# Layer 1's fifth modulation chunk, moved from the second attention to the boundary between the layers

## The reference, cut to what matters

```python
for l in range(DEPTH):                      # DEPTH = 2
    mod = (silu(c) @ w_ada[l] + b_ada[l])   # 6 x 1024 values, and the same for c_ctx
    sh1, sc1, gt1, sh2, sc2, gt2 = jnp.split(mod, 6, axis=-1)
    h = modulate(rms_norm(x, g_mix[l]), sh1, sc1)
    ... = split_in(h @ w_in[l])             # conv, neighbourhood attention, windowed attention, gates
    x = x + gt1 * merge_branches((o_a, o_b, o_c), (ga, gb, gc), w_branch[l], w_out[l])
    h = modulate(rms_norm(x, g_ffn[l]), sh2, sc2)
    x = x + gt2 * expert_choice_ffn(h, w_router[l], w_exp_gate[l], w_exp_up[l], w_exp_down[l])
```

## Time and profile before

| what | value |
|---|---|
| median of 3 runs | 1836.38 us (1835.15 to 1837.97) |
| the profiled execution | 1836.14 us, span 1834.3 us |
| TensorE busy | 1686.4 us, 92% |
| VectorE busy | 765.9 us, 42% |
| ScalarE busy | 476.6 us, 26% |
| read from HBM | 539.13 MB, 296 GB/s over the span |

### The profile page before, as it was taken

The page is one execution under the profiler, slowest core; times in us unless marked ns, Lnnn a source line. Parts: engine busy times, 40 slices in busy tenths (PEclk is TensorE's granted clock), DMA queues, the critical chain, the costliest instruction groups (busy, mean ns, idle before and its releaser), DMA issues.

```text
span 1834.3 us, 26452 instructions
## 1 busy us (share of the span) xinstructions
PE 1686.4 (92%) x10822; PEld 974.9 (53%) x10822; DVE 765.9 (42%) x1742; ACT 476.6 (26%) x1048; POOL 109.5 (6%) x149
## 2 busy tenths in 40 slices
PE   5999999999998999999998799999999998787876
PEld 3887777776664333333232498877882332222222
DVE  3455566665424233332323665577753222111111
ACT  4224455552133100000000535555441000000001
POOL 1101210000001000000000012200000000000000
PEclk9999999999998999999999999999999999999988
DMA  9533231127778999999999774247899999999997
GB/s 351 159 92 95 84 92 58 37 79 262 268 274 350 409 428 427 428 428 427 428 427 427 275 226 132 76 132 261 284 366 381 426 426 426 427 424 426 426 426 288
DMA packets 149987, 543.83 MB, mean 296 GB/s; under 512 B 10026, under 2 KB 88304, under 8 KB 124652
## 3 DMA queue, kind: packets, MB, share of 16 engines
q1 hardware_dynamic: 147056, 535.35, 74.5%
q0 software_dynamic: 2400, 6.16, 1.3%
q10 hardware_dynamic: 412, 0.64, 0.1%
HBM read 539.13 MB, written 2.98 MB: 296 GB/s over the span
## 4 chain that ended last, share of the span: by engine, by line
PE 67%; DMA 25%; DVE 3%; ACT 2%; SPq 1%; issue 1%; POOL 0%; DVEq 0%; ACTq 0%
PE bank L2193 19%; PE bank L2053 11%; PE bank L2054 10%; PE bank L2055 10%; DMA ring<-in_w_exp_gate 8%; DMA ring<-in_w_exp_down 8%; DMA ring<-in_w_exp_up 5%; DMA spare<-in_w_exp_gate 3%; PE bank L1952 2%; PE bank L2082 2%; PE bank L2106 2%; PE bank L2167 2%; PE bank L2092 2%; PE bank L2222 1%; DMA ring<-in_w_in 1%
## 5 line engine op out<-in xcount | busy, mean ns | idle before, releaser
L2193 PE MATMUL bank<-ring,XEP 128*32 128x256 f32 (+1 forms) x2384 | 385.3, 618 | 32.0 <-DMA ring<-in_w_exp_gate 15.5
L2053 PE MATMUL bank<-HH,WH 128*128 128x512 f32 (+1 forms) x800 | 286.4, 358 | 4.8 <-DVE HL L1642 4.0
L2054 PE MATMUL bank<-HL,WH 128*128 128x512 f32 (+1 forms) x800 | 275.4, 344 | 0.0
L2055 PE MATMUL bank<-HH,WL 128*128 128x512 f32 (+1 forms) x800 | 274.9, 344 | 0.0
L2193 PEld LDWEIGHTS bank<-ring,XEP 128*32 128x32 f32 (+1 forms) x2384 | 114.7, 130 | 272.3 <-issue 226.4
L1614 DVE TENSOR_TENSOR WL<-ring,WH 128x1024 fp32r<-128x1024 f32 (+1 forms) x172 | 184.6, 1076 | 139.9 <-ACT WH L1373 139.1
L1874 DVE TENSOR_TENSOR X<-X,bank 128x512 f32<-128x512 f32 x184 | 113.9, 681 | 185.9 <-PE bank L2222 100.2
L1373 ACT CAST WH<-ring 128x1024 fp32r<-128x1024 f32 (+1 forms) x172 | 158.0, 926 | 126.4 <-PE bank L2055 64.7
L2193 PE MATMUL bank<-ring,HIDT 128*32 128x256 f32 (+1 forms) x1232 | 153.0, 479 | 31.1 <-DMA ring<-in_w_exp_down 31.1
L2053 PEld LDWEIGHTS bank<-HH,WH 128*128 128x128 f32 x800 | 151.7, 190 | 50.0 <-issue 26.7
L2055 PEld LDWEIGHTS bank<-HH,WL 128*128 128x128 f32 x800 | 151.8, 190 | 18.5
(11 more groups left out here) (251 smaller groups left out, 2050.8 us busy)
## 6 DMA issues: line engine op xcount, KB each, us to landing
ring<-in_w_exp_gate SPq DMA_DIRECT2D x55, 2048.0 KB, 31.0
ring<-in_w_exp_up SPq DMA_DIRECT2D x49, 2048.0 KB, 34.7
ring<-in_w_exp_down SPq DMA_DIRECT2D x48, 2048.0 KB, 36.3
ring<-in_w_ada SPq DMA_DIRECT2D x48, 1024.0 KB, 7.6
ring<-in_w_in SPq DMA_DIRECT2D x40, 1024.0 KB, 8.3
split_slot<-in_w_exp_up SPq DMA_DIRECT2D x8, 2048.0 KB, 29.1
split_slot<-in_w_exp_down SPq DMA_DIRECT2D x8, 2048.0 KB, 33.3
ring<-in_w_in SPq DMA_DIRECT2D x28, 512.0 KB, 5.2
```

The lines of the kernel that those rows point to most:

```text
L2053: mm(t, wh, hi[:, k, 0:b.n], start=k == 0, stop=False)
L2054: mm(t, wh, lo[:, k, 0:b.n], start=False, stop=False)
L2055: last = mm(t, wl, hi[:, k, 0:b.n], start=False, stop=k == b.kk - 1)
L2193: last = mm(out_bank[tw * g:tw * g + tw, 0:nw], stationary(k), w[:, g::G] if spread else w[:, nw * g:nw * g + nw], start=k == 0, stop=k == ...
```

## The change

Chunk 4 of layer 1 is no longer made in the second attention. Its two pieces are loaded between the two loads of the first products ("ac"), at the layer's head. TensorE multiplies the first half (four matmuls) into bank 3 ahead of the turns, once four of the last eight additions to X are done, and the second half behind the first five turns. VectorE copies it after the first two product blocks, and its transposes follow the third. The second attention's four pairs then carry chunks 5, 6, 7 and 8, one each; before they carried 4, then 5 and 6, then 7, then 8.

```diff
+GT1_0 = 2 * GT1
+    def boundary_ada(l, c, pieces):
+        mm = P.tile(dve=True, bank=3)
+        for ch in pieces:
+            ch.used_tile = mm.ready
+        return Step(kind="ada", layer=l, l=l, v=c // 2, half=c % 2, chunk=pieces, tile=mm, buffer=0)
...
-            return [P.load([(0, (8, 256), ("w_in", l, COL[name] + 256 * r, 256))]) for r in range(2)]
+            between = []
+            if last and name == "ac":
+                between = [(0, (4, 512), ("w_ada", l, 512 * GT1_0, 512, 4 * r, 4)) for r in range(2)]
+            first, second = [(0, (8, 256), ("w_in", l, COL[name] + 256 * r, 256)) for r in range(2)]
+            loaded = [P.load([part]) for part in [first] + between + [second]]
+            return loaded[:1] + loaded[-1:], loaded[1:-1]
+
+        boundary = None
+        if l == 0:
+            turns = turn_steps(0, KD // 2)
+        else:
+            first_ac, pieces = col_chunk("ac")
+            turns = turn_steps(0, 5)
+            boundary = boundary_ada(l, GT1_0, pieces)
+            turns += turn_steps(5, KD)
...
                 elif turns:
+                    P.add("ada_part", ada=boundary, halves=(0,))
                     P.steps[l] += turns[:5]
+                    P.add("ada_part", ada=boundary, halves=(1,))
                     for k, (one, two) in enumerate(zip(ksteps(P, head), ksteps(P, b))):
...
                     run([("done", head), ("done", b)])
+                    P.add("ada_out", ada=boundary)
+                    turn_ada(boundary)
...
-                now = ((4,), (5, 6), (7,), (8,))[p]
-                sums = sums[:mid] + [("call", ada(l, now[0]))] + sums[mid:] + [("call", ada(l, c)) for c in now[1:]]
+                sums = sums[:mid] + [("call", ada(l, GT1_0 + 1 + p))] + sums[mid:]
...
+                    elif kind == "ada_part":
+                        if 0 in s.halves:
+                            pe.wait_ge(x_added, ADD0[l] - ADDS[l - 1] + 4)
+                        modulation(s.ada, s.halves)
```

More of the change, by code:

```diff
@@ L96, with __init__ @@
 class Step:
-    def __init__(self, ac_tile=None, act=None, after_expert=None, arrive=None, arrived=None, at=None, b=None, bank=None, before=None, bias=None, buffer=None, casts=None,
+    def __init__(self, ac_tile=None, act=None, ada=None, halves=None, after_expert=None, arrive=None, arrived=None, at=None, b=None, bank=None, before=None, bias=None, buffer=None, casts=None,
                  bias_before=None, blk=None, br=None, c_tile=None, chunk=None, code=None, col=None, d=None, d_tile=None,
@@ L109, in __init__ @@
         self.act = act
+        self.ada = ada
+        self.halves = halves
         self.after_expert = after_expert
@@ L372, in ada, with turn_ada, turn @@
         return go
+    def boundary_ada(l, c, pieces):
[3 more added lines that the diff above has]
+        return Step(kind="ada", layer=l, l=l, v=c // 2, half=c % 2, chunk=pieces, tile=mm, buffer=0)
+    def turn_ada(s):
+        def turn():
+            s.out = [P.tile(dve=True)]
+            P.mods += 1
+            P.add("ada2", l=s.l, v=s.v, half=s.half, out=s.out, tile=s.tile, buffer=s.buffer)
+        P.deferred.append(turn)
     def window_load(l, c):
@@ L418, in turn_steps @@
             return [Step(kind="trmod", layer=l, which=0, k=k, ntt=4, tile=P.tile(act=True), mods=P.mods, hts=8 * l + k) for k in range(first, end)]
-        turns = turn_steps(0, KD if l else KD // 2)
         def col_chunk(name, l=l):
-            return [P.load([(0, (8, 256), ("w_in", l, COL[name] + 256 * r, 256))]) for r in range(2)]
+            between = []
[12 more added lines that the diff above has]
+            turns += turn_steps(5, KD)
         ac_tiles = []
         for name in ("ac", "ax", "ab"):
-            ch = first_ac if l == 0 and name == "ac" else col_chunk(name)
+            ch = first_ac if name == "ac" else col_chunk(name)[0]
             for i in range(KB):
@@ L1617, in _ @@
                         nc.vector.tensor_copy(MB[s.buffer][:], BLK[s.tile.bank][:]).then_inc(dve_evicted, 1)
+                    elif kind == "ada_out":
+                        dve.wait_ge(blk_ready, s.ada.tile.ready)
+                        nc.vector.tensor_copy(MB[s.ada.buffer][:], BLK[s.ada.tile.bank][:]).then_inc(dve_evicted, 1)
                     elif kind == "ada2":
```

## The result

| | before | after |
|---|---|---|
| median | 1835.57 us, 5 runs (1835.15 to 1837.97) | 1845.20 us, 5 runs (1841.77 to 1846.28) |
| ratio | | 1.0050, 95% interval 1.0039 to 1.0062 |
| profiled execution, span | 1836.14, 1834.3 us | 1845.96, 1844.2 us |

The kernel is 9.6 us slower by the medians.

The account below looks back on a forecast made before the run. Layer 1's expert weight stream was taken to set the end: a 12.3 us later stream less 1.8 us gained gives +10.5 us, 1846.9 us on the median of 1836.38; range 1842 to 1851 us for 8 in 10.

Parts of the forecast that it names:

- The bound: Layer 1's experts: the end is set by when their weight stream is through; TensorE idles 65.7 us from 1510 to 1810.
- Removed: Second attention of layer 1: one chunk's matmul passes (1.85 us) and four transposes (0.48 us) leave TensorE's chain, 2.33 us.
- Added at the boundary: Between the layers: both halves taken as 0, ends +0.4 and -0.3; four transposes after the third product block, +0.48 us.
- g: Gain that reaches layer 1's experts: 2.33 - 0.48 = 1.85 us, taken as 1.8, with ends of 1.1 and 2.2.
- The ring, the wait, the hole: Before layer 1's experts: modulation chunk 11 in slot 0 holds expert chunks 6 to 10; transfers stand from about 1369 to 1383.
- the sum: Shift of expert chunk 16's landing, layer 1: 1440.3 - 1428.0 - g = 12.3 - 1.8 = +10.5 us.
- First landing: Expert chunk 6 after the hole: 2 MB on an idle queue take 8.1 us, landing at 1391.0 - g.
- The ten chunks behind it: Layer 1's expert stream: ten steps of 4.93 us, so chunk 16 lands at 1440.3 - g.
- the old gaps stay: Rival, behind expert chunk 10: freed slots come too late, +10.5 + 4.8, 1851.7 us; chance 0.04.
- w_out's later wait: Layer 1's dense part: w_out's first half also waits for two later blocks' splits; up to 8 us costs nothing.
- The hole is hidden: Rival, the other side: TensorE's backlog from 1380 to 1510 us covers the late chunks, 1834.6 us; chance 0.08.
- Only partly there: Rival: slot 0 is freed earlier or loads move faster than 425 GB/s; +4 to +6, 1841 to 1843 us; chance 0.04.

Follow-up runs that it names:

- a_swap: Changed kernel with modulation chunk 10 in slot 0 and chunk 11 in slot 2, so expert chunk 6 waits for chunk 10; 1844.76 us, 1.0048 of before.
- a_late: Changed kernel in which expert chunk 6 also waits for a tile of the selection, ready a little after the modulation; 1849.05 us, 1.0068 of before.
- a_fix: Changed kernel with the last two modulation chunks placed by hand so that slot 0 is free of them; 1833.69 us, 0.9986 of before.
- b_hole: Kernel before, with only modulation chunk 11 placed in slot 0 and chunk 10 in slot 1; 1847.82 us, 1.0066 of before.
- a_fix_early: As a_fix, with both halves of the moved chunk ahead of the turns; 1833.34 us, 0.9987 of before.
- a_order: Changed kernel with layer 1's last five first expert loads issued in the order 9, 7, 8, 10, 6; 1833.62 us, 0.9988 of before.
- a_order_early: As a_order, with both halves of the moved chunk ahead of the turns; 1832.83 us, 0.9981 of before.

## Why the prediction was right

**The bound.** "The end of the kernel is set by when layer 1's expert stream is through." It holds: the last product waits for a transfer in both kernels, and the end followed the issue of the late load nearly one for one over after, a_swap and a_late.

**Removed: 2.33 us predicted.** Counted from S, chunk 4's leaving the second attention is worth 2.44: layer 1 is 0.56 us late at the second chunk of that attention (220.03 to 220.59) and 1.88 early at the next that both have there (242.91 to 241.03). The stretch of the earlier trace rows is as full as before, 40.00 of 40.00 us.

**Added at the boundary: 0.48 us predicted, with ends.** In this trace the term was a little small. I took the second half at 0 with an upper end of +0.4, and the first half's burst as perhaps holding the clock (-0.3). The burst didn't hold it: the granted clock was 0.50 when the turns began. The Trainium skill ("TensorE: Matmul & The Clock Gate", section "Why this matters for your kernels") says that gaps between bursts drop the clock; by that rule, the trace agrees, since the burst left a gap of 5.49 us and the clock fell in it. I had taken that filling the stretch in part might be enough, and had said that by that rule the -0.3 would hold; that was a misreading, since the rest of the stretch is still such a gap. The upper end of +0.4 was too low for this trace: it counted the half alone at the lower clock, and the turns ahead of it ran at that level to their end and were 0.29 us longer than before (4.50 for 4.21). With the half at 1.82 us, ScalarE's wait at 0.86 and the MB transposes at 0.66, the first product of the third block starts at S + 23.68 instead of 22.83, 0.85 later. By the second attention 0.56 of it is left. So g = 2.44 - 0.56 = 1.88 at the load of gt2's bias (S + 272.57 to 270.69), where I had 1.8. It is not that exact: the five kernels with this boundary issue that load at S + 270.24 to 270.94, so g is 1.6 to 2.3 by the trace, and the close match is in part luck.

**The ring, the wait, the hole.** As predicted in place and cause. The queue's wait is 26.8 us, not "about 13": I took the wait for as long as the hole, and SyncE issues ahead of the landings, so it begins to wait while 15 us of transfers are still under way. The last piece is issued at 1350.91 and lands 15.2 us later, at 1366.1. The hole in the transfers, from there to about 1381, is some 15 us against the 14 that I had. This slip changed no term of the sum.

**First landing.** 8.1 us predicted, 7.3 measured. The other loads of 2 MB that found the queue idle so took 7.3 to 7.5: chunk 6 in a_late (7.3), b_hole and a_swap (7.5), chunk 9 in a_fix and a_fix_early (7.4). Chunk 6 lands at 1387.95, S + 358.85; predicted was 1389.2, S + 359.36. The estimate of 6.8 us from the Trainium skill ("DMA: Bandwidth & Descriptors", section "Anatomy of one DMA — SWDGE (gpsimd) path") is 0.5 too low for this load; the page's fit is for transfers that GpSimd issues, and this one is SyncE's. My value was 0.8 too high; no row of before had quite this case.

**The ten chunks behind it.** 10 x 4.93 = 49.3 us predicted; from 1387.95 to chunk 16's landing at 1438.4 they are 50.5. The stream was not slower: from 1388 to 1438 us it moved 427 GB/s, by which ten chunks take 49.1 us (an estimate from that figure). Other loads' bytes must have passed in between; which, no row shows. The freed slots did come in time (rival "the old gaps stay" is out): the share is 1.01 from 1386 on. Chunk 16 lands at S + 409.32, against S + 398.15 before: +11.2 where the sum said +10.5: 0.5 less for the earlier first landing, 1.2 more for the ten steps.

**w_out's later wait.** Its first half is issued at 1321.81, S + 292.71 (before S + 286.40), and lands 8.1 us later instead of 16.4, because the queue ahead is nearly empty (the DMA share is 1.00 until 1322 and 0.51 in the half microsecond after). Its first cast at 1334.89 is 1.88 us earlier from S than before. It costs nothing, as taken.

**From +11.2 to +9.6.** The last product is 11.3 us later from S. Layer 0 was 0.74 us shorter in the profiled execution of after, and the kernel's end comes 0.7 us sooner behind the last product (13.0 us, before 13.7): the granted clock under the last scatters was 0.51 in before's trace (1822 to 1825 us) and 1.00 in after's (1833 to 1836). That leaves the spans 9.9 apart, and the medians 9.6. I had neither in the sum; they are within the spread of the runs (1841.77 to 1846.28). The sum's +10.5 lies between the +11.3 of the traces and the +9.6 of the medians; that the forecast of the time is as near as it is owes something to that.

**The other side.** "The hole is hidden" is refuted by b_hole. "Only partly there" is out by the stretch from 1366 to 1380 us with a share of 0.00 (its price was also added up loosely: +4 to +6 on 1836.4 is 1840.4 to 1842.4, not 1841 to 1843). The rival of the experiments, that a part of the loss is the boundary's, is refuted by a_fix: with all of the boundary in place it is faster than before.

So the chunk's move is worth some 2 us of gain (2.2 by the medians of a_fix, 0.9 to 4.0 by its interval), and the place where the ring put an unrelated load cost 11.5 to 12. a_fix, a_fix_early, a_order and a_order_early are each 0.1 to 0.2% faster than before, with intervals that leave out 1, and so faster than after. At 1832.8 to 1833.7 us they can't be told apart.

## What to carry to other kernels

When a change adds or removes a load near the head of a ring or another rotating buffer, follow the new positions to the last load and list what each waits for; the load to look at is the one whose wait got longer and that has ready loads behind it in an in-order queue. Its own lateness cost nothing here, and what it held up cost 11.5 us: put loads whose buffers are free ahead of it, or give the late user a slot whose next load comes later. And count two traces from an event that the change can't have moved, else the drift of an untouched stage hides or fakes a microsecond or two.

## What the runs showed of the hardware

Four things that I had not expected. A burst of 1.07 us of matmuls in an idle stretch of 8 us did not keep the clock for the turns, nor did one of 1.92 us in a_fix_early, which left 4.62 us: its granted clock is 0.50 from 1043 to 1044 us as well. When the clock comes back differs between executions of the same instructions: five traces have the same boundary, and the half chunk between the turns took 1.06 to 1.82 us in them. A 2 MB load that found the queue idle landed after 7.3 to 7.5 us in six kernels; behind the hole, five such loads issued within 2.5 us landed the last one 26.2 us after its issue, at 428 GB/s from 1386 to 1410 us. And the issuing queue's wait (26.8 us) is no measure of the transfers' idle time (15 us): the difference is the backlog that was in flight when the wait began.
